# Latent attention: products over 128 rows, three score buffers, and gating work and row roots moved

## What is computed

```python
p = x @ w_in                                   # 528 x 1440, cut into gate, rec, q, kv, kpe
y_rec = lru(conv(p_rec)) * gelu(p_gate)        # recurrence over 528 tokens, 512 channels
q  = rmsnorm(p_q)  @ w_uq                      # 256 -> 8 heads x 96, last 32 rotated
kv = rmsnorm(p_kv) @ w_ukv                     # 128 -> 8 heads x (64 keys + 64 values)
k  = concat(kv[..., :64], rope(p_kpe))         # the 32 rotated columns are shared by the heads
o  = softmax(causal(q @ k.T / sqrt(96))) @ v
mix = concat(y_rec, o) @ w_out
```

## Time and profile before

| | us |
|---|---|
| median of 3 runs | 3287.14 |
| lowest and highest | 3284.31, 3288.56 |
| the profiled execution, its own time | 3288.93 |
| its span, first to last instruction | 3287.1 |
| gate tiles, 94.5 to 133.6 | 39.1 |
| attention, 133.6 to 294.3 | 160.7 |

### The profile page before, as it was taken

How to read it: one execution, slowest core, us unless ns; L and a number is a source line. 1 busy time by engine, 2 the same in 40 slices (tenths; PEclk the granted TensorE clock), 3 DMA queues, 4 the chain that set the end, 5 groups by cost and what they waited for, 6 DMA issues and landing times.

```text
span 3287.1 us, 42420 instructions
## 1 busy us (share of the span) xinstructions
PE 2953.0 (90%) x17555; PEld 2285.1 (70%) x17555; DVE 1430.0 (44%) x2508; ACT 912.2 (28%) x1628; POOL 601.0 (18%) x530
## 2 busy tenths in 40 slices
PE   7889999999999899999998898888698897988884
PEld 6647999998888678888787455555576675555552
DVE  4643432334444443233445443333497845533334
ACT  3433422323222334132322111111335621211111
POOL 1201300112111122012100442222000003522220
PEclk9969999999999999999999899999899998999997
DMA  4020222222222123222223999999621119999996
GB/s 135 14 64 27 78 91 90 90 90 87 68 72 76 52 77 103 90 94 98 77 90 132 375 408 409 409 409 409 212 70 61 37 31 370 406 408 410 408 409 267
DMA packets 272068, 600.31 MB, mean 183 GB/s; under 512 B 32631, under 2 KB 177458, under 8 KB 255482
## 3 DMA queue, kind: packets, MB, share of 16 engines
q1 hardware_dynamic: 247408, 569.47, 46.1%
q0 software_dynamic: 23968, 27.93, 2.6%
q10 hardware_dynamic: 490, 0.08, 0.0%
HBM read 607.75 MB, written 39.89 MB: 197 GB/s over the span
## 4 chain that ended last, share of the span: by engine, by line
PE 82%; DVE 7%; issue 4%; DMA 3%; ACT 2%; SPq 1%; POOL 1%; ACTq 0%; DVEq 0%; POOLq 0%
PE ps L101 77%; PE ps L104 5%; DMA sb_ring<-in_exp_w_dram 1%; DVE sb_tmpA L118 1%; SPq L144 1%; DVE sb_arena L126 1%; DMA sb_hx<-in_exp_w_dram 1%; DVE sb_tmpA L126 1%; DVE sb_ws L118 1%; DVE sb_arena L118 1%; DVE sb_tmpA L129 1%; POOL sb_arena L118 1%; DMA sb_arena<-x_rows,sb_smallu 0%; DVE sb_tmpA L2095 0%; DVE sb_tmpA L122 0%
## 5 line engine op out<-in xcount | busy, mean ns | idle before, releaser
L101 PE MATMUL ps<-sb_hs,sb_ws 128*128 128x264 f32 (+1 forms) x6384 | 1107.0, 335 | 16.6 <-ACT sb_hs L108 7.1
L101 PEld LDWEIGHTS ps<-sb_hs,sb_ws 128*128 128x128 f32 x6384 | 972.1, 190 | 147.6 <-issue 14.0
L118 DVE TENSOR_TENSOR sb_ws<-sb_ring,sb_ws 128x1024 fp32r<-128x1024 f32 x279 | 370.8, 1333 | 432.8 <-ACT sb_ws L112 432.4
L101 PE MATMUL ps<-sb_arena 128*64 128x256 f32 (+16 forms) x2052 | 398.9, 440 | 53.8 <-issue 29.5
L112 ACT CAST sb_ws<-sb_ring 128x1024 fp32r<-128x1024 f32 x279 | 290.9, 1046 | 344.7 <-PE ps L101 329.9
L101 PE MATMUL ps<-sb_ring,sb_arena 128*64 128x256 f32 (+2 forms) x2314 | 321.6, 432 | 54.4 <-issue 50.7
L101 PE MATMUL ps<-sb_br,sb_ws 128*128 128x264 f32 (+1 forms) x2304 | 366.5, 321 | 0.0
L101 PEld LDWEIGHTS ps<-sb_br,sb_ws 128*128 128x128 f32 x2304 | 332.3, 188 | 33.7
L101 PEld LDWEIGHTS ps<-sb_arena 128*64 128x64 f32 (+6 forms) x2052 | 229.6, 163 | 179.9 <-issue 98.8
L101 PEld LDWEIGHTS ps<-sb_ring,sb_arena 128*64 128x64 f32 (+1 forms) x2314 | 194.4, 147 | 147.9 <-issue 83.2
L108 ACT ACTIVATE sb_arena<-ps 64x256 f32<-64x256 f32 (+6 forms) x188 | 73.7, 403 | 792.4 <-PE ps L101 762.8
(11 more groups left out here) (189 smaller groups left out, 2182.8 us busy)
## 6 DMA issues: line engine op xcount, KB each, us to landing
sb_ring<-in_exp_w_dram SPq DMA_DIRECT2D x160, 1024.0 KB, 21.2
sb_hx<-in_exp_w_dram SPq DMA_DIRECT2D x128, 1024.0 KB, 21.5
sb_arena<-in_exp_w_dram SPq DMA_DIRECT2D x96, 1024.0 KB, 21.2
sb_ring<-in_mlp_w_dram SPq DMA_DIRECT2D x64, 1024.0 KB, 5.2
sb_ring<-in_od_w_in_dram SPq DMA_DIRECT2D x24, 1024.0 KB, 5.3
sb_ring<-in_conv_w_in_dram SPq DMA_DIRECT2D x12, 1024.0 KB, 5.0
sb_ring<-in_attn_w_in_dram SPq DMA_DIRECT2D x10, 1024.0 KB, 5.1
sb_ring<-in_od_w_out_dram SPq DMA_DIRECT2D x8, 1024.0 KB, 4.8
```

The costliest lines, as they stand in the source:

```text
L101: return self.e.matmul(o, l, r, start=start, stop=stop, skip_group_check=True)
L118: return self.e.tensor_tensor(o, a, b, op)
```

## The change

1. **128 rows.** `turn`, `s` and `t` contract over all 128 rows of `QH` and `KT`. POOL sets rows 96 to 127 of `QH` to zero (after the recurrence), and in `more_rows_pool` rows 96 to 127 of `KT` to zero and row 96 to one, for heads 0 to 3 ahead of the four `y` products and for heads 4 to 7 after the rotation product of head 1. `QH`, `Vt`, `triT` and `PT` change places in SBUF.
2. **Score buffers.** Blocks 0 and 1 of a head (16 and 128 queries) share one step and one PSUM bank. Blocks 0 to 3 go to a ring of two single banks, block 4 to a place of its own (`last`, which also takes `l`): three buffers in place of two. The negative maxima of blocks 0 and 1 are one instruction.
3. **Order of the attention.** The key product is a step of its own (`k`), and so is the sum of the rotation (`rot`). The copy of the rotated keys moves from DVE to ACT. The halves of the recurrence output are steps (`mix`) amid the first two heads.
4. **Roots.** All three squares are taken before the gate tiles, each in a buffer of its own; `rms_pe` runs for both q and kv inside the first pair of gate tiles (at k = 4), and both roots are taken ahead of the first gelu.

```diff
+            def roots():
+                rms_pe(e, side, "q")
+                rms_pe(e, side, "kv")
...
-            for m in dense(e, "win", CX[4:], 8, even_x, T1, main):
-                if m < 2:
-                    rms_pe(e, side, ("q", "kv")[m])
+            for m in dense(e, "win", CX[4:], 8, even_x, T1, main, True, roots):
...
+            squares_act(e, "q")
+            squares_act(e, "kv")
             for m in range(4):
                 split_hi(e)
+                if m == 0:
+                    rms_act(e, "q")
+                    rms_act(e, "kv")
                 e.wait_ge(*summed["win", m])
...
+            e.wait_ge(*dve_lru["h", 3])
+            e.wait_ge(*pool_lru["b", 3])
+            e.mset(QH[96:128, :, :], 0.0).then_inc(*pool_rot.mark("qrows"))
+            e.wait_ge(*pool_rot["qrows"])
+            more_rows_pool(e, 0)
...
+            yield from (("q", 0), ("k", 0), ("q", 1), ("k", 1), ("turn", 0), ("q", 2), ("k", 2), ("rot", 0), ("turn", 1),
+                        ("mix", 0), ("q", 3), ("rot", 1), ("mix", 1))
             for h in range(4):
...
+                yield from (("s", 5 * h), ("turn", h + 2), ("s", 5 * h + 2), ("k", h + 3), ("rot", h + 2))
                 yield "s", 5 * h + 3
+                if h < 2:
+                    yield "mix", h + 2
+                yield from (("s", 5 * h + 4), ("q", h + 4))
+            yield from (("ln", 0), ("turn", 6), ("k", 7), ("v", 0), ("rot", 6), ("turn", 7), ("lse", 0), ("v", 1), ("rot", 7),
+                        ("l", 0), ("v", 2), ("v", 3), ("v", 4))
+            for i in (0, 2, 3, 4):
+                yield "s", 20 + i
+            late = [5 * h + i for h in (5, 6, 7) for i in (0, 2, 3, 4)]
             for k in range(26):
...
+                for x in late[2 * k:2 * k + 2]:
                     yield "s", x
...
-            rows = Ring([PS[2], PS[3]], U_, emptied)
+            rows = Ring([BANK[4], BANK[5]], U_, emptied)
+            last = Ring([PS[3]], U_, emptied)
...
-                        t = e.mm(o, rmat[0:96, 0:96], QH[0:96, x, a:b], True, True)
+                        t = e.mm(o, rmat[:, 0:96], QH[:, x, a:b], True, True)
...
+                                t = e.mm(v[0:tn, lo:hi], QH[:, h, t0:t0 + tn], KT[:, h, lo:hi], True, True)
...
-                    K, Q1 = KT[0:97, h, :], QH[0:97, h, :]
+                    K, Q1 = KT[:, h, :], QH[:, h, :]
...
+                    e.acp(halves(KT[0:64, x, :]), whole(U_["kh", x], T1, 0, 64)).then_inc(*act_emptied.mark())
+                    e.acp(KT[64:96, x, :], kpe[64:96, :]).then_inc(*act_emptied.mark(("kh", x)))
...
-                    e.cp(KT[64:96, x, :], kpe[64:96, :]).then_inc(*dve_soft.mark(("kpe", x)))
...
+        def more_rows_pool(e, g):
+
+            k = KT[96:128, 4 * g:4 * g + 4, :]
+            e.mset(k, 0.0).then_inc(*pool_rot.mark())
+            e.wait_ge(*pool_rot.now)
+            e.mset(k[0:1], 1.0).then_inc(*pool_rot.mark(("krows", g)))
+            e.wait_ge(*pool_rot["krows", g])
```

More of the change, by code:

```diff
@@ L618, in rms_pe @@
             u = side.take(e, ("rms", what))
-            srcs = RMS[what][0]
-            for i in range(len(srcs)):
+            squares = RMS[what][2]
+            for i, sq in enumerate(squares):
                 e.wait_ge(*act_lru["sq", what, i])
                 for o, a, b in split(u, T1):
-                    t = e.mm(o, ones, SQ[i][:, a:b], i == 0, i == len(srcs) - 1)
-                t.then_inc(*normed.mark(("rms", what, i)))
+                    t = e.mm(o, ones, sq[:, a:b], i == 0, i == len(squares) - 1)
+            t.then_inc(*normed.mark(("rms", what)))
         def even_pe(e, units):
@@ L655, in gates_act, with squares_act, rms_act @@
                     *act_emptied.mark((g, c)))
[L657 to L662, removed]
+        def squares_act(e, what):
+            xs, _, squares, _ = RMS[what]
+            for i, x in enumerate(xs):
                 emptied(e, ("win", (8, 9, 10)[(what == "kv") * 2 + i]))
                 e.wait_ge(*dve_init["tmp"])
-                e.act(SQ[i], x, ACT.Square).then_inc(*act_lru.mark(("sq", what, i)))
-            e.wait_ge(*normed["rms", what, len(srcs) - 1])
-            e.act(halves(MU), whole(U_["rms", what], T1), ACT.Sqrt, scale=1.0 / n, bias=eps5).then_inc(
+                e.act(squares[i], x, ACT.Square).then_inc(*act_lru.mark(("sq", what, i)))
+        def rms_act(e, what):
+            _, n, _, root = RMS[what]
+            e.wait_ge(*normed["rms", what])
+            e.act(halves(root), whole(U_["rms", what], T1), ACT.Sqrt, scale=1.0 / n, bias=eps5).then_inc(
                 *act_emptied.mark(("rms", what)))
@@ L702, in even_act @@
                     *act_emptied.mark(("win", m)))
[L703 to L709, removed]
         def even_dve(e):
@@ L805, in program @@
         ar.at = base0
+        Vt = ar.take(5, 512)
+        triT = ar.take(128)
+        PT0 = ar.take(1360)
+        ar.at = base0 + 8 * T1
         QH = ar.take(8, T1)
-        Vt = ar.take(5, 512)
-        PT = ar.take(2, 1360)
-        triT = ar.take(128)
+        PT = (PT0, ar.take(1360))
         LROW = tmpA[0:4, 2:4, :]
@@ L854, in mla_order @@
                     yield "lse", 1
-                for _ in range(3 - k % 2 if k < 6 else 0):
+                for x in late[2 * k:2 * k + 2]:
                     yield "s", x
-                    x += 1
                 if k == 5:
@@ L923, in mla_pe @@
                         rows.drain(e)
+                        last.drain(e)
                         held = cols.holder
@@ L973, in mla_act @@
                     e.acp(halves(QH[0:96, x, :]), whole(U_["qh", x], T1, 0, 96)).then_inc(*act_emptied.mark(("qh", x)))
-                    e.wait_ge(*summed["kh", x])
-                    e.acp(halves(KT[0:64, x, :]), whole(U_["kh", x], T1, 0, 64)).then_inc(*act_emptied.mark(("kh", x)))
+                if step == "k":
+                    if x == 0:
+                        e.wait_ge(*dve_lru["kpe"])
+                    if x >= 4:
+                        e.wait_ge(*pool_lru["y", 3])
+                    e.wait_ge(*summed["kh", x])
+                    e.acp(halves(KT[0:64, x, :]), whole(U_["kh", x], T1, 0, 64)).then_inc(*act_emptied.mark())
+                    e.acp(KT[64:96, x, :], kpe[64:96, :]).then_inc(*act_emptied.mark(("kh", x)))
+                if step == "mix":
+                    e.wait_ge(*summed["win", 3])
+                    e.wait_ge(*pool_lru["y", x])
+                    e.acp(HS[:, 0, x, :], XC[:, x, :]).then_inc(*x_hi.mark(("mix0", x)))
                 if step == "v":
                     tn = TT[x][1]
+                    e.wait_ge(*x_lo["mix0", 3])
                     e.wait_ge(*summed["vt", x])
                     e.acp(Vt[0:tn, x, :], U_["vt", x][0:tn, 0:512]).then_inc(*act_emptied.mark(("vt", x)))
-                if step == "s":
+                for x in blocks_of(step, x):
                     h, i, t0, tn, n = qblock(x)
```

88 lines of the change are left out of this document (44 added, 44 removed).

## The result

The median of four runs of the changed kernel is 3241.86 us (3238.10 to 3244.11), against 3287.85 us (3284.31 to 3291.53) of the kernel before. The ratio is 0.9859, with a 95% interval of 0.9847 to 0.9870. The forecast was 3241. The profiled execution took 3244.11 us, where the sum of the steps said 3242.9.

What follows compares the result with a forecast made beforehand. PE was taken as the bound, losing time to waits and a low clock. Terms summed to -48.7 us; 2.7 us for dips left -46.0, 3242.9 against 3288.93; with the median 1.8 us lower, 3241 us, range 3227 to 3260.

Steps and rivals of the forecast that it cites:

- Gate tiles: Gate tiles: PE no longer waits for squares and roots, end near 122.9 us instead of 132.9, -10.0 us.
- Opening: Start of the attention, now with a fourth head's query product: 13.6 us against 13.10, +0.5 us.
- Loop: Four-head attention loop: PE becomes the bound at 7.6 us a head, 30.4 us for 50.50, -20.1 us.
- Tail: End of the first half, after the loop: about 12.1 us for 14.5, DMA issues still in the way, -2.4 us.
- Head 4: Head 4 after the tail: three buffers and a rising clock, 6.0 us for 8.70, -2.7 us.
- one or two dips: Allowance of 2.7 us for falls of the clock, as PE still waits for DMA issues in the tail.
- Mixed stretch: Scores of three heads with t and o products, at the high clock: 21.5 us for 35.50, -14.0 us.
- The rest: Last window of 38.40 us, already at the high clock, and everything later: unchanged, moves up whole, 0 us.
- A: Rival: rows, or zero rows, don't count; head 4 and mixed stretch stay at 1.2 GHz, 3258 us, chance 0.15.
- B: Rival: a PE wait per head stays in the loop, 9.6 us a head, +8, 3249 us, chance 0.10.
- C: Rival: slower, clock low from opening to end of attention as twelve-record groups are split, 3309 us, chance 0.04.
- D: Rival: gain given back later, output layer or weight load not ready, at most some 20 us, 3261, chance 0.05.

Runs made afterwards that it cites:

- e4: Changed kernel with the roots change undone (squares, sums and roots again after gate tiles 0 and 1): 3254.19 us, ratio 0.9901.
- e5: Changed kernel with only the score buffers undone, all blocks in one ring of the two old two-bank places: 3246.12 us, ratio 0.9862.
- e6: Changed kernel with only the old order inside the attention loop restored: 3248.89 us, ratio 0.9878.
- e7: Changed kernel with the four small DMAs of each log-sum step issued by POOL instead of ACT: 3239.22 us, ratio 0.9844.
- e1: Changed kernel with its old row counts, turn and s over 96 rows and t over 97: 3249.76 us, ratio 0.9899.
- e2: Changed kernel with turn, s and t over 97 rows: 3249.18 us, ratio 0.9882.
- e3: Kernel before with the 128-row change alone (zero rows, moved tiles; old buffers, order and roots): 3278.23 us, ratio 0.9971.
- e10: The kernel of e3 run a second time, for a second profile: 3281.78 us.

## Why the prediction was right, step by step

**Right, with one reason overrated.** The forecast was 3241 against 3241.86. The terms hold one by one, within 3.1 us each, and their errors cancel to 0.4 us at the output layer; with a spread of 6.0 us between runs, the agreement within 1 us is luck. The rows were the right cause for terms 5 and 6, but they carry only 6.9 of the 16.7 us that the working laid to them.

1. *Gate tiles.* -9.6 for -10.0; no wait over 1 us, as said. e4 gives 9.1 for this part by itself.
2. *Opening.* 13.9 for 13.6 us.
3. *Loop.* 29.5 for 30.4 us, at 1.00. The reading that the third buffer and the products between the blocks both go at the latency of mask, maximum and exponential was right. What it didn't say is that either alone does most of it: of their 21.1 us together, 17.0 stay without the third buffer (e5) and 13.5 without the order (e6).
4. *Tail.* 12.6 for 12.1 us. The DMA issues on ACT were named as the wait that stays, and e7 shows them to be worth 2.6 us.
5. *Head 4* was mis-sized: 7.6 us for 6.0. The working had a clock that rises within it, and it was at 0.50 until 186.4 us. The 2.7 us set aside for "one or two dips" cover these 1.6, but not the 4.3 us given back later as well.
6. *Mixed stretch.* 18.4 us, below the lower bound of 20. Of the 3.1 us too much, 0.9 was put down for waits, and the one row with a wait there shows 0.4. Another 0.7, by my estimate, is the count of heads: the stretch has 12 of the 64 wide `o` records, 1.5 heads, with two heads of `t`, not 1.85 of both. A head of scores was put at 3.1 us, and in the timeline of the loop above it takes about 2.8, which is another 0.9 for three heads. The rest, about 1 us, I haven't traced. With 1.6 too little in head 4, two errors met.
7. *The rest.* 39.2 for 38.40 us, and the 4.3 us of above, against a forecast of zero.

**The rivals.** A is excluded as a mechanism (e1, e2), but its price was the weaker part: with the old rows the changed kernel takes 3249 to 3250 us, not 3258. I had laid the whole gain of head 4 and the mixed stretch to the rows. Without them e1 still takes only 38.5 us from head 4 to the log sums, where the kernel before took 49.7. One argument for the rows was a coincidence, too: before, the clock rose about when the last 96-row block was done, but in e1 it rises at 201.7 us, in the middle of the 96-row blocks, and stays up. B's wait moved to ACT's copies, as it said it could, but costs 0.8 us a head and not 2.6. C needed a low clock in the loop: with the twelve-record groups split up it stayed at 1.00, in e1 also. D's size, 4.3 us, is within the spread.

## What to carry to other kernels

Where PE reads busy and its clock 0.50, look for products that contract over fewer than 128 rows: rows of zeros cost their memset and nothing on PE, and they brought the clock back sooner here. The rows were worth 12.8 to 16.6 us with the old waits and 6.9 with the new order, so count them after the waits that let the clock fall, not before. Where a ring of banks holds PE, a further bank and other work in the gap are two ways to one gain; count it once.

## What the hardware showed that I had not expected

- **The clock comes back later over 96 rows than over 128, with the same busy share.** After the dip behind the logarithm it came back 20.9, 22.8, 15.6 and 6.4 us after the start of head 4 with 96, 97, 112 and 128 rows, PE busy 86% or more of each. Over 128 rows with the old order and two buffers it was 8.3 and 14.3 us (e3, e10), over 96 rows with these 42.8.
- **POOL beside DVE.** A `y` product on POOL took 1.31 us before, where DVE stood idle, and 2.10 us after, where DVE was at products of its own (116.64 to 119.61 us); the reason is not shown.

```profile
107.00 1.31 POOL L118 TENSOR_TENSOR sb_arena<-sb_arena 128x528 f32<-128x528 f32 x1 [7.83 <-ACT sb_arena L108]
```

```profile
116.95 2.10 POOL L118 TENSOR_TENSOR sb_arena<-sb_arena 128x528 f32<-128x528 f32 x1 [3.22 <-ACT sb_arena L108]
```

- **A memset of POOL by shape.** One of 32 rows by 4224 columns with two smaller ones took 7.46 us for the 7.2 forecast: the 32 rows cost as much as the one of the earlier trace rows.
